# Gate and up weights of each expert laid beside each other, and loaded by partition halves

## The reference

```python
for e in range(N_EXPERTS):                                   # 32
    he = jax.nn.silu(t @ w_gate[e]) * (t @ w_up[e])          # w_gate[e], w_up[e]: 1024 x 256
    y = y + combine[:, e, None] * (he @ w_down[e])           # w_down[e]: 256 x 1024
```

## Time and profile before

| | us |
|---|---|
| median of three runs | 710.69 |
| the profiled execution, its own time | 712.32 |
| its span, first to last instruction | 710.6 |
| TensorE matmuls busy | 661.0 (93%) |
| VectorE, ScalarE, GpSimd busy | 240.0, 121.8, 65.2 |
| SyncE's transfers (queue q1), share of 16 engines' span | 95.6% |
| moved | 273.30 MB, mean 385 GB/s |

### The profile page before, as it was taken

The page is one execution under the profiler, slowest core; times in us unless marked ns, Lnnn a source line. Parts: engine busy times, 40 slices in busy tenths (PEclk is TensorE's granted clock), DMA queues, the critical chain, the costliest instruction groups (busy, mean ns, idle before and its releaser), DMA issues.

```text
span 710.6 us, 12991 instructions
## 1 busy us (share of the span) xinstructions
PE 661.0 (93%) x4808; PEld 402.3 (57%) x4808; DVE 240.0 (34%) x649; ACT 121.8 (17%) x317; POOL 65.2 (9%) x187
## 2 busy tenths in 40 slices
PE   4889999999888888896999999998999999999995
PEld 1445465555554555453888788776555555455552
DVE  0114423222222222233296495235322223223233
ACT  4113430000000000012233233138000000000003
POOL 7000021111101001000000000000111101111100
PEclk9999999999999999999999999999999999999999
DMA  8999999999999999999989998993899999999992
GB/s 344 409 418 412 415 415 419 414 417 419 416 419 417 417 420 417 417 417 395 369 322 335 394 308 359 365 376 147 344 417 415 418 416 414 420 415 416 418 410 89
DMA packets 61207, 273.30 MB, mean 385 GB/s; under 512 B 4452, under 2 KB 18276, under 8 KB 39656
## 3 DMA queue, kind: packets, MB, share of 16 engines
q1 hardware_dynamic: 61016, 272.39, 95.6%
q10 hardware_dynamic: 144, 0.26, 0.1%
HBM read 271.59 MB, written 1.05 MB: 384 GB/s over the span
## 4 chain that ended last, share of the span: by engine, by line
PE 79%; DMA 9%; issue 3%; ACT 3%; DVE 2%; POOLq 1%; SPq 1%; POOL 1%; DVEq 0%; ACTq 0%
PE bank L684 70%; PE bank L882 8%; DMA ring<-in_ada_w_dram 8%; ACT reg_a L1401 1%; DMA ring<-in_w_o_dram 1%; POOLq L642 1%; POOL xh L643 1%; PE bank L1211 1%; DVE ring L1727 1%; SPq L420 0%; ACT hx L1684 0%; DVE nmx L2136 0%; DVE reg_c L1727 0%; DVE ye L1727 0%; ACT reg_b L1509 0%
## 5 line engine op out<-in xcount | busy, mean ns | idle before, releaser
L684 PE MATMUL bank<-ring,xh 128*64 128x256 f32 (+1 forms) x2496 | 336.5, 424 | 16.6 <-issue 13.5
L684 PEld LDWEIGHTS bank<-ring,xh 128*64 128x64 f32 x2496 | 187.5, 138 | 121.6 <-issue 56.4
L643 POOL COPY xh<-reg_a 128x256 f32 (+1 forms) x130 | 51.9, 400 | 464.1 <-PE bank L684 323.5
L1420 ACT ACTIVATE reg_c<-bank 128x128 f32<-128x128 f32 x64 | 17.8, 278 | 396.0 <-PE bank L684 396.0
L1724 DVE TENSOR_TENSOR reg_c<-reg_c,bank 128x128 f32<-128x128 f32 x64 | 18.4, 288 | 193.9 <-ACT reg_c L1420 193.9
L882 PE MATMUL bank<-ye,reg_b 32*128 32x512 f32 (+1 forms) x528 | 64.8, 602 | 0.0
L684 PE MATMUL bank<-reg_b,ring 128*128 128x256 f32 x256 | 58.5, 386 | 0.9 <-ACT reg_b L1552 0.9
L684 PE MATMUL bank<-ring,cact 128*32 128x512 f32 (+1 forms) x320 | 40.4, 614 | 20.0 <-DMA ring<-in_ada_w_dram 19.9
L1724 DVE TENSOR_TENSOR ye<-bank,reg_c 128x512 f32<-128x512 f32 (+1 forms) x66 | 44.3, 671 | 35.4 <-PE bank L684 34.5
L684 PEld LDWEIGHTS bank<-reg_b,ring 128*128 128x128 f32 x256 | 49.2, 194 | 7.7 <-issue 1.1
L1937 DVE COPY xh<-bank 128x128 f32<-128x128 f32 x64 | 18.3, 285 | 96.3 <-PE bank L684 96.3
(11 more groups left out here) (167 smaller groups left out, 393.7 us busy)
## 6 DMA issues: line engine op xcount, KB each, us to landing
ring<-in_exp_w_gate_dram SPq DMA_DIRECT2D x62, 1024.0 KB, 17.2
ring<-in_exp_w_up_dram SPq DMA_DIRECT2D x62, 1024.0 KB, 19.1
ring<-in_exp_w_down_dram SPq DMA_DIRECT2D x62, 1024.0 KB, 20.6
ring<-in_ada_w_dram SPq DMA_DIRECT2D x48, 1024.0 KB, 15.8
ring<-in_w_qkv_dram SPq DMA_DIRECT2D x12, 1024.0 KB, 13.6
ring<-in_w_o_dram SPq DMA_DIRECT2D x4, 1024.0 KB, 7.1
hx<-in_x_dram SPq DMA_DIRECT2D x1, 1024.0 KB, 5.3
gu_spare<-in_exp_w_gate_dram SPq DMA_DIRECT2D x1, 1024.0 KB, 12.5
```

What stands on the lines that cost most here:

```text
L643: nc.gpsimd.tensor_copy(xe[:, b, k0:k1, t * CAP:(t + 1) * CAP], hS[:, k0:k1, bass.ds(off, CAP)])\
L684: return nc.tensor.matmul(o_, l_, r_, start=start, stop=stop)
L1420: nc.scalar.activation(sil[:, b, :], bank[b][:, 0:P], ACT.Silu).then_inc(S("sil_ready", L), 1)
```

## The change

On the host, before the launch, gate and up of each expert are laid into one array `exp_w_gate_up` of shape (2, 32, 128, 4096): for each expert and partition 8 KB of gate followed by 8 KB of up. An expert's gate and up, 2 MB, are then contiguous in HBM. On the device `gate_up` issues two transfers of 1 MB as before, but the first takes partitions 0 to 63 with 16 KB each (it adds to `ring_first`), the second partitions 64 to 127 with 16 KB each (`ring_mid`). `gate_part`, `up_part` and the overflow path keep their code; `gate_d` and `up_d` are now column slices of the new array, so that their 8 KB runs stand 16 KB apart in HBM. Where data lies in SBUF is as before, and so are all waits and all matmuls.

```diff
+def beside(exp_w_gate, exp_w_up):
+
+    parts = [np.asarray(a).reshape(2, E, P, 1, W2) for a in (exp_w_gate, exp_w_up)]
+    return np.ascontiguousarray(np.concatenate(parts, 3).reshape(2, E, P, 2 * W2))
...
-        gate_d = exp_w_gate.rearrange("l e (p k) f -> l e p (k f)", k=KC)
-        up_d = exp_w_up.rearrange("l e (p k) f -> l e p (k f)", k=KC)
+        gate_d, up_d = exp_w_gate_up[:, :, :, 0:W2], exp_w_gate_up[:, :, :, W2:2 * W2]
...
             def gate_up(L, e, s, freed):
                 if s < R:
                     sp.wait_ge(S("ring_free", s), freed)
-                gate_part(L, e, s)
-                up_part(L, e, s)
+                for p0, name in ((0, "ring_first"), (P // 2, "ring_mid")):
+                    rows = slice(p0, p0 + P // 2)
+                    sp.dma_start(gate_up_w(s)[rows, :], exp_w_gate_up[L][bass.ds(e, 1), rows, :].rearrange("a p n -> (a p) n"))\
+                        .then_inc(S(name, s), 16)
```

More of the change, by code:

```diff
@@ L119, in program @@
 def program(nc, x, c, ada_w, ada_b, norm_mix_g, norm_ffn_g, pool_w, pool_scale, w_qkv, w_o,
-            router_group_w, router_expert_w, exp_w_gate, exp_w_up, exp_w_down, final_norm_g,
+            router_group_w, router_expert_w, exp_w_gate_up, exp_w_down, final_norm_g,
             vecs, router, gbias, misc, out):
@@ L2214 @@
 _INS = ["x", "c", "ada_w", "ada_b", "norm_mix_g", "norm_ffn_g", "pool_w", "pool_scale", "w_qkv", "w_o",
-        "router_group_w", "router_expert_w", "exp_w_gate", "exp_w_up", "exp_w_down", "final_norm_g"]
+        "router_group_w", "router_expert_w", "exp_w_gate_up", "exp_w_down", "final_norm_g"]
 def kernel(**inputs):
@@ L2224 @@
     nc = _bacc.Bacc("TRN2", target_bir_lowering=False, num_devices=1, dynamic_dma_scratch_size=1024)
+    inputs = dict(inputs, exp_w_gate_up=beside(inputs["exp_w_gate"], inputs["exp_w_up"]))
     arrays, args = {}, {}
```

## The result

The changed kernel takes 1146.8 us (four runs, 1122 to 1163), the kernel before 711.4. The ratio, 1.585 (95% interval 1.572 to 1.598), takes the two faster runs alone, 1122 and 1133 us, and the profile is of one of the two slower ones, 1161 us. The kernel is slower by far, in the direction of the forecast and beyond its range (787 to 1008). The profiled execution has a span of 1159.0 us, 448 more than before.

The account below looks back on a forecast made before the run. Transfers were taken to bound layer 0's experts, transfers and TensorE together layer 1's. 710.6 + 146 (layer 0) + 5 (between) + 106 (layer 1) = 967.6 us of span, median set at 968 us, range 787 to 1008.

Parts of the forecast that it names:

- What bounds the kernel: Expert stages: transfers alone set layer 0's pace, 15.06 us per two experts; in layer 1 TensorE and transfers are both at their limit.
- Issues, semaphores, experts 10 and 17, the layout: Same issues, semaphores, waits and SBUF layout; layer 1's experts 10 and 17 keep 8 KB runs 16 KB apart; cost 0.
- Fewer packets: Gate and up transfers: four 16 KB runs per engine for eight of 8 KB, 13.7 ns saved each, 2.45 us for 2.51.
- Half the partitions: Each gate and up half: ends 2.45 us (engine's own pace) and 4.79 (shared ways into SBUF); 4.79 taken, doubled half 0.60.
- All engines work through one queue in the same order: DMA queue: engines are in the low half together, then the high half; an expert takes 2 x 4.79 + 2.51 = 12.1 us.
- rival 1: Expert transfers: halves share ways only in part as engines drift apart; 789 us at a third of the loss, chance 0.20.
- My sign of 250 to 270 GB/s: Layer 0's expert stretch in the changed profile should move 250 to 270 GB/s at a DMA share near or above 1.
- predicted 146: Layer 0's experts: 64 halves, each 4.79 us instead of 2.51, add 146 us.
- Between the stages: Between the expert stages: ten queued halves, some lengthening the w_o wait; +5 us taken, ends 0 and +14.
- Layer 1's experts: Layer 1's expert stage: 25 remaining experts at 12.1 us each; the stage grows by 106 us, span 967.
- TensorE's clock: TensorE in the expert stages, idle half the time, may get a lower clock; 0 taken, up to some 20 us.
- The range: Whole kernel: 787 us (a third of the loss) to 1008 (doubled halves, overheads not hidden, some clock cost).

Follow-up runs that it names:

- whole_down: As whole, with the down weights also laid out on the host so that a partition's 8 KB are one run instead of two of 4 KB; 705.9 us.
- columns: The changed kernel's new array, but two transfers over all 128 partitions with 8 KB runs, gate then up; 711.4 us.
- landed: The changed kernel with SyncE's layer 0 loop written out, waiting after each expert's issues until its down weights have landed; 1142.1 us.
- drain_even_odd: The changed kernel with even and odd partitions for the halves, SyncE waiting in layer 0 after each expert's issues until its down product is done; 926.9 us.
- halves_l1: The changed kernel with partition halves in layer 1 only and one whole 2 MB transfer per expert in layer 0; 920.9 us.
- whole: The changed kernel with one 2 MB transfer per expert over 128 partitions, 16 KB runs, in place of the two halves; 709.2 us.

## Why the prediction was wrong

*What bounds the kernel.* Right. Layer 0's experts follow the transfers alone (whole_down shortens them and only them: its layer 1 takes 704.2 - 488.9 = 215.3 us from the same mark, to the tenth what it took before), and in layer 1 a slower transfer costs nearly all that it adds.

*Issues, semaphores, experts 10 and 17, the layout.* Cost 0, as said; columns shows it.

*Fewer packets.* The mechanism holds, with 9 ns for the 13.7 ns per packet. Packets fell as predicted.

*Half the partitions.* The choice between the ends was right, and nearly the size: 4.79 us predicted. From an empty queue, landed shows 13.6 us from issue to the down landing and drain_even_odd 9.2, so 2.2 more for each half than its 2.45, 4.65. In a full queue the first expert's halves moved 208 and 196 GB/s, 5.0 to 5.35 us each. The 6.5 GB/s for each partition should have been 6.7 (1.0486 MB in 2.45 us over 64); nothing rested on it. The Trainium skill's page "SBUF — State Buffer", section "Door 1: The DMA port swizzle", named in the prediction, gives 196 GB/s for 1 MiB into partitions 0 to 63 and about 218 for long transfers. The trace agrees roughly: 196 to 208 in the full queue, 225 by the 4.65 us.

*The step that failed* is "All engines work through one queue in the same order, each with its share of every transfer, so they are in the low half together and then in the high half together", with what followed from it, 2 x 4.79 + 2.51 = 12.1 us. The term that it gets wrong is the 2.51 us of the down transfer behind the halves; the halves themselves, at 5.0 to 5.35 us, would make up only 0.4 to 1.1 of the 2.3 us that are missing. In the steady state the down transfers go at half rate as well, and an expert takes 14.4 us at 218 GB/s. The first expert takes about 14 already. From an emptied queue a group takes 12.9 us of DMA time, near the 12.1. I had named drift in rival 1, but took it for a relief between my sum and the old time; if it is drift, it is a loss beyond it. Whether it is drift stays open. My sign of 250 to 270 GB/s failed on the low side, where I had named no rival. With 14.4 in the same sum, layer 0 grows by 32 x (14.4 - 7.53) = 220 us; measured 218.0, predicted 146.

*Between the stages.* +11.1 measured, +5 taken, 0 to 14 given. The `w_o` wait is 19.18 us for 8.72: the halves queued ahead of it, as the prediction had it.

*Layer 1's experts.* Same sum: 499 + 229 + 25 x 14.4 + 14.7 = 1103 for the end, against 967 predicted and 1159 in the profile. Of the 56 us that are left, 41 are the rate of 196 GB/s, 16.05 us per expert (25 x 1.65); the rest I put down to the emptier queue late in the stage (share 0.96), which no run isolates. Other executions of the changed kernel are nearer to the sum, with spans of 1120.5 and 1131.2. In halves_l1, at 208 to 212 GB/s or 15 us per expert and with its second mark 6 us later than before (501.19), the sum gives 499 + 6 + 25 x 15 + 14.7 = 895 for a span of 907.6.

*TensorE's clock.* It fell to 0.79 of full speed over the expert stages, low and high level in turns. A second bound it was not: TensorE is busy 0.59 to 0.62 of the time, and the DMA engines are full (1.01 and 1.02).

*The range* ended at 1008, because its upper end added only small costs to 12.1 us. The bound that the same reasoning offered was all three transfers at half rate, 3 x 5.02 = 15.1 us per expert, or 499 + 241 + 5 + 25 x 15.06 + 14.7 = 1136 us. I left it out by trusting that engines stay in step, for which I had no row. It is 11 us under the measured 1147.

## What to carry to other kernels

Where transfers are the bound, each should reach to both sides of partition 64. If it must be split, split it into even and odd partitions (708 us here) or along the free dimension, as gate and up in columns (711 us), not into 0 to 63 and 64 to 127 (1147 us). A DMA share of 1 says that engines are occupied, not that bytes move: read it together with GB/s. When transfers of two kinds share a queue, price the slow kind also for what it does to the others, and let the bound of the range be the whole mix at the slow rate.

## What the runs showed of the hardware that was not expected

64 partitions are enough for the full rate: 422 GB/s with even and odd, as in whole with all 128. With halves in the queue, full-width transfers slow down too, to 196 to 228 GB/s for all together; started together with its halves on an empty queue, a down transfer reached 370. Emptying the queue after each expert, which leaves the DMA engines idle for 13 to 16% of the stage, cost only 19.7 us in layer 0. And kernels with halves repeat badly: 1122 to 1163, 1100 to 1174 and 932 to 987 us, against under 1% for full-width ones. Why stays open.
